# A hybrid decoder step on one core: x's norm weights in a transfer of their own, and one k tile of u's second group ahead of the first state products

## The reference, cut to what matters here

```python
def rmsnorm(x, g):
    r = lax.rsqrt(jnp.mean(xf * xf, axis=-1, keepdims=True) + EPS)
    return xf * r * g

z = rmsnorm(x, p['attn_norm_g']) @ p['w_in']          # 2048 -> q 1024, k 256, v 256, u 1024
q, k, v, u = split_projection(z)
attn = window_attention(rmsnorm(q, ..), rmsnorm(k, ..), v)
# state-space half: 64 groups of 16 channels, 64 complex states each
bu = einsum('ntgh,gph->ntgp', u, B_bar);  h = scan(A_bar, bu);  y = real(C h) + D u
ssm_out = g * sigmoid(g @ w_glu + b_glu)              # g = gelu(y)
h = x + concat(rmsnorm(attn), rmsnorm(ssm_out)) @ w_out
y = h + square(relu(rmsnorm(h) @ w_mlp_up)) @ w_mlp_down
```

## Time and profile before

| | us |
|---|---|
| median of 3 runs | 1183.04 (1181.49 to 1183.18) |
| the profiled execution | 1182.39 |
| its span, first to last instruction | 1180.6 |
| PE busy | 1173.7 (99% of the span) |
| DVE busy | 750.3 (64%) |
| ACT busy | 426.1 (36%) |

### The profile page before, as it was taken

How to read it: one execution, slowest core, us unless ns; L and a number is a source line. 1 busy time by engine, 2 the same in 40 slices (tenths; PEclk the granted TensorE clock), 3 DMA queues, 4 the chain that set the end, 5 groups by cost and what they waited for, 6 DMA issues and landing times.

```text
span 1180.6 us, 20253 instructions
## 1 busy us (share of the span) xinstructions
PE 1173.7 (99%) x8492; PEld 1104.1 (94%) x8492; DVE 750.3 (64%) x759; ACT 426.1 (36%) x515; POOL 137.0 (12%) x83
## 2 busy tenths in 40 slices
PE   9999999999999999999999999999999999999998
PEld 7677576799999999999999999999999999999998
DVE  7899899899776565545456554545554545565454
ACT  6110012975544333333333433333433333433331
POOL 0421503000000000100000100000110000110000
PEclk9999999999999999999999999999999999999999
DMA  7443334434455444455455455545445545445553
GB/s 290 157 135 112 112 125 140 166 107 159 146 170 188 162 170 168 155 174 172 161 164 173 145 181 171 166 161 169 153 157 187 173 162 163 159 150 185 173 170 117
DMA packets 55192, 190.29 MB, mean 161 GB/s; under 512 B 7864, under 2 KB 10168, under 8 KB 54712
## 3 DMA queue, kind: packets, MB, share of 16 engines
q1 hardware_dynamic: 54824, 188.79, 47.9%
q10 hardware_dynamic: 288, 0.30, 0.1%
HBM read 185.82 MB, written 5.28 MB: 162 GB/s over the span
## 4 chain that ended last, share of the span: by engine, by line
PE 94%; DVE 4%; issue 1%; ACT 1%; DMA 0%; SPq 0%
PE psum L1370 93%; DVE states L745 1%; DVE turn L745 1%; DVE states L934 1%; DVE out_turn L745 0%; DVE out_turn L976 0%; PE psum L1489 0%; DMA small<-in_small 0%; ACT gate L606 0%; DVE q_t L994 0%; ACT L531 0%; DVE q_t L745 0%; ACT au L554 0%; DVE carry_p L745 0%; DVE kv_t L1028 0%
## 5 line engine op out<-in xcount | busy, mean ns | idle before, releaser
L736 DVE TENSOR_TENSOR w_lo<-w_raw,w_hi 128x1024 fp32r<-128x1024 f32 x292 | 407.1, 1406 | 385.4 <-ACT w_hi L450 384.7
L1370 PE MATMUL psum<-mov_b,w_hi 128*128 128x288 f32 x2624 | 522.3, 295 | 0.3 <-ACT gate L606 0.3
L450 ACT ACTIVATE w_hi<-w_raw 128x1024 fp32r<-128x1024 f32 x292 | 306.5, 1059 | 481.0 <-PE psum L1370 480.3
L1370 PEld LDWEIGHTS psum<-mov_b,w_hi 128*128 128x128 f32 x2624 | 419.8, 188 | 1.6 <-issue 0.7
L1370 PE MATMUL psum<-mov_a,w_hi 128*128 128x288 f32 x2048 | 406.6, 295 | 0.0
L1370 PE MATMUL psum<-mov_b,w_lo 128*128 128x288 f32 x1312 | 385.4, 294 | 0.0
L1370 PEld LDWEIGHTS psum<-mov_a,w_hi 128*128 128x128 f32 x2048 | 327.7, 188 | 0.1
L1370 PE MATMUL psum<-mov_a,w_lo 128*128 128x288 f32 x1024 | 300.7, 294 | 0.0
L1370 PEld LDWEIGHTS psum<-mov_b,w_lo 128*128 128x128 f32 x1312 | 247.6, 189 | 0.0
L1370 PEld LDWEIGHTS psum<-mov_a,w_lo 128*128 128x128 f32 x1024 | 193.3, 189 | 0.0
L1370 PE MATMUL psum<-x_g,w_raw 128*128 128x288 f32 x640 | 163.5, 413 | 0.6 <-ACT x_g L460 0.6
(11 more groups left out here) (182 smaller groups left out, 517.7 us busy)
## 6 DMA issues: line engine op xcount, KB each, us to landing
w_raw<-in_w SPq DMA_DIRECT2D x335, 512.0 KB, 3.3
h_t<-in_x SPq DMA_DIRECT2D x3, 576.0 KB, 8.8
out_y<-h_t SPq DMA_DIRECT2D x3, 576.0 KB
b_w<-in_b SPq DMA_DIRECT2D x1, 1024.0 KB, 5.8
c_w<-in_c SPq DMA_DIRECT2D x1, 1024.0 KB, 7.2
k_cache<-in_kc SPq DMA_DIRECT2D x1, 1024.0 KB, 5.7
v_cache<-in_vc SPq DMA_DIRECT2D x1, 1024.0 KB, 7.8
out_kc<-in_kc SPq DMA_DIRECT2D x1, 992.0 KB
```

What stands on the lines that cost most here:

```text
L450: nc.scalar.activation(hi3[:, n % SLOTS, :], raw3[:, n % SLOTS, :], ACT.Copy) \
L736: nc.vector.tensor_tensor(lo3[:, n % SLOTS, :], raw3[:, n % SLOTS, :], hi3[:, n % SLOTS, :].bitcast(F32), ALU.subtract) \
L1370: return nc.tensor.matmul(out, lhs_t, rhs, start=start, stop=stop)
```

## The change

Two edits. First, `g_in` (16 columns, 64 bytes on each partition, 8 KB) leaves the transfer of `small` and becomes a transfer that ACT issues between the two tiles of x, with a semaphore of its own. ACT then scales tile 0 first, and does the Exp of `log_dt` after it. Second, k tile 0 of u1 is issued ahead of the first pair, each round's k tile is m + 1 instead of m, and the run behind the rounds begins at 9.

```diff
+        gains_loaded = sem("gains_loaded")
...
-            sp.dma_start(small[:, 0:first], ins["small"][:, 0:first]).then_inc(small_loaded, 16)
+            rest = slice(SMALL["g_in"].stop, first)
+            sp.dma_start(small[:, rest], ins["small"][:, rest]).then_inc(small_loaded, 16)
...
             act.dma_start(h_t[:, 0:TOK], ins["x"][:, 0:TOK]).then_inc(x_first, 16)
+            act.dma_start(small[:, SMALL["g_in"]], ins["small"][:, SMALL["g_in"]]).then_inc(gains_loaded, 16)
             act.dma_start(h_t[:, TOK:2 * TOK], ins["x"][:, TOK:2 * TOK]).then_inc(x_second, 16)
+            act.wait_ge(gains_loaded, 16)
+            gain_x(0)
             act.wait_ge(small_loaded, 16)
             nc.scalar.activation(disc3[:, DT, :], small[:, SMALL["log_dt"]], ACT.Exp).then_inc(disc_fun, 1)
-            gain_x(0)
             gain_x(1)
...
             pe.wait_ge(b_loaded, 16)
+            gemm_full("g_u1", S_U1, GROUP_STEPS, xg3, part=range(1))
             for m in range(HALF_PAIRS // 2):
                 project_pair(0, 2 * m)
                 project_pair(0, 2 * m + 1)
-                gemm_full("g_u1", S_U1, GROUP_STEPS, xg3, part=range(m, m + 1))
-            gemm_full("g_u1", S_U1, GROUP_STEPS, xg3, part=range(8, KT))
+                gemm_full("g_u1", S_U1, GROUP_STEPS, xg3, part=range(m + 1, m + 2))
+            gemm_full("g_u1", S_U1, GROUP_STEPS, xg3, part=range(9, KT))
```

## The result

The changed kernel took **1184.65 us** (median of 21 runs, 1183.79 to 1187.08) against 1183.03 us for the kernel before (21 runs, 1181.42 to 1184.85). The ratio is 1.0012, 95% interval 1.0007 to 1.0018: slower by about 1.4 us, clear of noise, yet under the 0.2% that the prediction set as its limit. The forecast was 1183.8, +0.8. Slower, and by under 0.2%, is what was forecast; the sum was too small by about half, and one of its terms had the wrong sign.

A forecast was written before the change was run, and what follows sets the result against it. PE bounds the kernel, on the last-ending chain for 94% of the span. The terms -0.13 + 1.26 - 0.42 + 0.10 sum to +0.81 us, giving a forecast median of 1183.8 us, range 1182.3 to 1185.1.

The forecast's parts named there:

- I take -0.13 us: Kernel start: PE's first real matmul 0.26 us earlier, worth -0.13 us, with -0.44 and +0.12 as ends.
- a table load slips in: Rival at ACT's start: Copy and Exp need two tables, a 1.28 us load delays Exp; +1.5 us, 1184.5; chance 0.06.
- The landing: Kernel start: the 8 KB norm-weight transfer lands at 4.5 us, between 4.3 and 4.9.
- The cover: Before u0's read-out: DVE's 1.03 us wait for PE hides its roughly 0.3 us later start; 0.6 left, no cost.
- PE's pause: Behind u0: PE idles 1.66 us instead of 0.60, as tile 0 waits for all four read-out pieces.
- The tile ahead of pair 0: Before round 0: k tile 0 of u1 takes 2.14 us ahead of pair 0.
- The net of wait and moved tile, with round 1: Rounds: pair 0 +3.21 us later, one tile less behind (-1.95), net +1.26; cheaper round 1 gives -0.42.
- The last product with C: Later in the kernel: DVE's lateness exceeds its 0.68 us slack there; +0.1 us, between 0 and 1.0.
- a stage further on collides: Rival: DVE late in the turn-outs or second half's rounds, up to +1 us more, 1184.8; chance 0.10.
- The clock rises earlier: Rival at the start: a shorter pause before the first real matmul brings full pace sooner; 1183.3; chance 0.15.
- The clock falls in the new pause: Rival behind u0: 1.66 us of idle PE drops the clock to half pace; +2.7 us, 1185.7; chance 0.05.
- It does what it is for: Rival behind u0: the tile runs in the pause without waiting for the read-out; -0.5 us, 1182.5; chance 0.04.

The follow-up runs named there:

- e3: Kernel before plus only the norm-weight transfer and tile 0 scaled first, both tile 0 transfers on one semaphore: 1183.99 us, lowest time +0.45 us.
- e5: Changed kernel with tile 0's two transfers on one semaphore, so the table load stands ahead of the waits: 1183.83 us.
- e1: Kernel before plus only the norm weights' own transfer and tile 0 scaled before the Exp: 1183.24 us, lowest time +1.30 us.
- e7: Kernel before with tile 0 scaled ahead of the Exp, one wait for x's tile 0 and `small`, no new transfer: 1184.14 us.
- e8: Kernel before with two more warm-up matmuls on zeros, eight of 288 columns instead of six: 1181.57 us.
- e2: Kernel before plus only k tile 0 of u1 issued ahead of the first pair: 1183.81 us, lowest time +1.11 us.
- e9: e8 plus k tile 0 of u1 ahead of the first pair, waiting for all four read-out pieces: 1182.61 us.
- e4: e2 with each matmul of k tile 0 waiting only for the read-out piece whose bank it writes: 1182.59 us, lowest time +0.06 us.
- e11: Changed kernel with six more warm-up matmuls: 1185.47 us, lowest time +2.48 us.
- e12: e8 plus k tile 0 of u1 ahead of the first pair, waiting piece by piece: 1181.49 us.
- e6: Changed kernel with tile 0's transfers on one semaphore and u1's k tile 0 waiting piece by piece: 1183.71 us, lowest time +0.39 us.
- e10: e1 with six more warm-up matmuls: 1182.90 us, lowest time +1.41 us.

## Why the prediction was right in direction and too small in size

**Edit 1, the step that failed.** "I take -0.13 us", with +0.12 as the dear end. Up to the end of u0 the profiled executions differ by +1.24 us. Three things stood in that term:

- The table load. The forecast held a rival, "a table load slips in", at 0.06, and argued against it by the functions: Copy and Exp share a table. No load was added; in that the trace agrees with the Trainium skill (ScalarE: Activation LUTs, Table sets), which has Copy in every set. What it didn't ask is where the one load would stand. It was visible in the profile of before, at 1.68 to 2.96, under ACT's wait for `small`; the change gave the first activation two waits. e3 shows its price, 0.85 us of the lowest time, and e5 against the changed kernel 0.88. The rival's sizes were near (DVE ready at 39.6, it was 39.44; 1184.5, it was 1184.65), its cause was not, so that is luck.
- The landing. 4.5 was taken for the 8 KB, between 4.3 and 4.9; it came at 4.7 (1.19 + 3.5) in the changed kernel and 4.8 in e3. The size says little here: 144 KB, 90 KB and 8 KB, issued at 0.74 to 1.2, all took 3.4 to 3.7 us. The Trainium skill (DMA: Bandwidth & Descriptors; the fit stands in its section Anatomy of one DMA, not in Bandwidth) has 2.0 us plus bytes over the rate, for GpSimd's path; the 8 KB on ACT's queue took 3.5 to 3.6. With 4.8 for 4.5 the whole gain of the transfer is gone even with the load in its place.
- The cover. "Cost nothing, as long as this cover holds", of the Exp behind tile 0. The cover of 1.03 us is there only where the clock rises late. In the traces with an early rise (e1, e5, e7, e8 and the later ones) the read-out begins without a wait for PE, and a later Exp shows in the time: e7, where DVE starts 0.50 us later, is at +0.39. The kernel before itself was not profiled with an early rise. A margin read in one execution was taken for a margin of the kernel.

**Edit 2, the steps that held.** PE's pause: 1.66 forecast, 1.69 measured. The tile ahead of pair 0: 2.14 and 2.11 (41.97 to 44.08). The net of wait and moved tile, with round 1: 1.26 - 0.42 = 0.84 forecast, 0.94 measured. Pairs 2 and 3 overlap (eight instructions from 47.39 in 2.06 us, where the earlier trace rows has 2.39). The last product with C: +0.1 forecast, 0.10 measured, DVE ending at 122.21 and PE beginning at 122.25; so the rival "a stage further on collides" did not come. e2 and e9 put the edit at 1.08 to 1.11 against the 0.94 of these terms, and e4 shows that the wait for the fourth piece is its cause.

**The rivals.** "The clock rises earlier" named a mechanism that e8 bears out, with the right cap by DVE, but it does not belong to this change, since edit 1 makes that pause longer, not shorter. "The clock falls in the new pause" had 0.05. In the changed kernel, seven of 21 runs lie at 1185.4 and above, with a mean clock of 0.999 or 0.997. For e5 and e11 the trace shows a fall of the clock inside or right behind just that pause, and of e9 and e12, which differ only in the wait, only e9 has an upper group; for the changed kernel itself no profiled execution caught a fall, so there it is an inference. What the forecast set against this rival, that the 0.6 us pauses were followed by full pace, holds only of the one behind u0: behind the one at the start PE ran at half pace. "It does what it is for" is refuted: even piece by piece the tile gains nothing (e4).

**The sum.** The measured ratio means +1.4 us where the lowest times say +2.4. That 1184.65 lies inside the range is in part luck: its upper end, 1185.1, was made of the collision further on, which did not come, and it covered the table load, which was not in the sum. The forecast's statement that the runs' spread was twice the effect was right, but it didn't ask what the spread was made of; the clock's groups take about 1 us of the difference back: 7 of 21 runs of the kernel before lie 3 us or so over its lowest time, in its dearest group, against 2 of 21 for the changed kernel. Which event makes that group is open. In e3 and e6 the granted clock fell to 0.50 at 263 us and 262 us, behind the products of 16 columns with v_cache; whether the kernel before's runs near 1184.6 all hold this fall was not shown.

## What to carry to other kernels

Count the waits in front of the first activation after a reordering. With one wait the table load stood ahead of it here, with two it went behind one of them, and 1.28 us that used to lie under a wait came onto the path, for 0.85 us of the time. Ask of each work put into a pause when the buffer that it writes is free: here the tile that should fill 0.6 us needed the last of four pieces, the work that it displaced only the first. Before shaving tenths at the start, look whether PE pauses between its warm-up and its first real work; two more warm-up matmuls, which took 0.27 us off such a pause, were worth 1.4 us in the median, more than either edit could have given.

## What the runs showed of the hardware that was not expected

- With 0.56 us or more between warm-up and first real matmul, PE came to full pace at 9 us or later in six of nine profiled executions, and at its first real matmul or close to it in three; with 0.40 us or less, and more warm-up work, it was there by about 7.4 us in all five. Ten of e8's eleven runs fell within 0.2 us of each other.
- The clock fell behind a pause of 2.5 us (e11) and inside one of 2.7 us (e5), and not behind pauses of 1.6 to 1.8 us in the profiled executions of the changed kernel, e2, e7, e9 and e10; in e1 it did fall, at 42.3, two us behind one of 1.6. The length of the pause alone does not decide.

```profile
42.30:45.60 3.30, 3.30 (x10) 2.00 (x10) 2.25 (x4) 1.91 (x3) 0.97 (x1) 0.50 0.00 0
```

- x's tile 1, moved from the second to the third place of ACT's queue (0.5 us later), landed at 6.2 us in the changed kernel (1.67 + 4.5) and at 7.9 in e1 (1.67 + 6.2), against 4.9 before. So it landed 1.3 to 3 us later for 0.5 us of later issue. Why is not shown; the 256 KB of `w_raw` that SP issued at the same moment took 4.3 and 6.0 us, against 3.9 before. In the changed kernel it was hidden, since PE needs that tile only after its first eight instructions.
